# Three rounded passes for the recurrence's projections, their low halves taken by VectorE between the convolutions, and two smaller moves beside them

## The reference

```python
h = _rmsnorm(x, attn_norm_w[l])
(g_qkv, g_z, g_b, g_a, d_q, d_k, d_v, c_q, c_k, c_v, gate_raw) = _split_cols(h @ w_in[l])
y_a = _gdn_mixer(g_qkv, g_z, g_b, g_a, ...)   # short convolution over 5 tokens, silu, l2norm, gated delta rule
y_b = _diff_mixer(d_q, d_k, d_v, ...)         # two softmax maps a head, 4 heads
y_c = _gqa_mixer(c_q, c_k, c_v, ...)          # 8 heads of grouped-query attention
merged = (gates[:, :, 0] * (y_a @ w_branch_a[l]) + gates[:, :, 1] * (y_b @ w_branch_b[l])
          + gates[:, :, 2] * (y_c @ w_branch_c[l]))
x = x + merged @ w_out[l]
x = x + _hier_moe(_rmsnorm(x, ffn_norm_w[l]), ...)  # top-1 group, top-2 of 8 experts, 32 experts of 1024 x 512 x 3
```

## Time and profile before

| | |
|---|---|
| median of 3 runs | 1626.24 us (1624.73 to 1628.49) |
| the profiled execution's own time | 1625.27 us |
| its span, first to last instruction | 1623.4 us |
| mean granted TensorE clock | 0.956 of full speed |
| busy: PE, PEld, DVE, ACT, POOL | 81%, 61%, 41%, 29%, 7% of the span |
| moved by DMA | 490.60 MB, mean 302 GB/s |

### The profile page before, as it was taken

One profiled execution on the slowest core, in us unless ns is written; L12 is line 12 of the kernel. 1 busy time (PEld: TensorE's weight loads), 2 busy tenths in 40 slices (PEclk: granted clock), 3 DMA queues, 4 the chain that ended last, 5 costly groups with the idle time before them and its releaser, 6 DMA issues. The chain is left out here.

```text
span 1623.4 us, 46306 instructions
## 1 busy us (share of the span) xinstructions
PE 1312.4 (81%) x19436; PEld 996.8 (61%) x19437; DVE 665.4 (41%) x1598; ACT 469.3 (29%) x968; POOL 120.7 (7%) x108
## 2 busy tenths in 40 slices
PE   6998899987777766677789979998877776766665
PEld 5787787765554544455577867887655554454444
DVE  6657756653222111111286667666522221111112
ACT  3446745441111000101145466454401111100101
POOL 2002530000000000000010035200000000000000
PEclk9998999999999998999999989999999999999998
DMA  9441024588999999999964210445899999999996
GB/s 343 167 148 52 14 100 174 194 362 362 425 425 428 430 428 428 429 429 427 410 221 156 104 57 2 156 158 218 347 400 405 426 428 428 428 428 428 429 428 267
DMA packets 76747, 490.60 MB, mean 302 GB/s; under 512 B 12878, under 2 KB 15462, under 8 KB 52070
## 3 DMA queue, kind: packets, MB, share of 16 engines
q1 hardware_dynamic: 76646, 489.16, 74.1%
HBM read 488.09 MB, written 1.05 MB: 301 GB/s over the span
## 5 line engine op out<-in xcount | busy, mean ns | idle before, releaser
L1969 PE MATMUL ps<-ring,arena 128*32 128x128 f32 x5632 | 195.3, 296 | 82.1 <-DMA ring<-in_expert_w_gate_dram 69.6
L1969 PEld LDWEIGHTS ps<-ring,arena 128*32 128x32 f32 x5632 | 172.1, 120 | 114.0 <-DMA ring<-in_expert_w_gate_dram 73.4
L2047 ACT ACTIVATE arena<-ps 128x128 f32<-128x128 f32 x66 | 18.3, 277 | 522.2 <-PE ps L1969 522.2
L2184 DVE TENSOR_SCALAR arena<-cst,arena 128x128 f32 x132 | 39.8, 344 | 233.6 <-issue 228.1
L468 POOL TENSOR_TENSOR small<-small,cst 128x8 f32<-128x8 f32 (+1 forms) x21 | 27.7, 1321 | 1242.7 <-DVE small L715 456.2
L1969 PE MATMUL ps<-arena 128*32 128x128 f32 x2688 | 90.9, 291 | 35.8 <-DMA arena<-in_expert_w_gate_dram 31.7
L1969 PEld LDWEIGHTS ps<-arena 128*32 128x32 f32 x2688 | 80.2, 117 | 49.2 <-DMA arena<-in_expert_w_gate_dram 37.0
L1935 PE MATMUL ps<-xn,arena 128*32 128x256 f32 x1088 | 74.7, 390 | 42.3 <-DVE arena L2130 41.2
L1741 DVE TENSOR_TENSOR w_low<-ring,w_high 128x512 fp32r<-128x512 f32 x126 | 85.8, 706 | 52.1 <-ACT w_high L1672 52.1
L1991 PE MATMUL ps<-ring,arena 128*32 128x256 f32 x1440 | 89.6, 388 | 13.2 <-DMA ring<-in_expert_w_down_dram 12.9
L1672 ACT ACTIVATE w_high<-ring 128x512 fp32r<-128x512 f32 x126 | 77.2, 634 | 74.5 <-PE ps L1608 62.2
(11 more groups left out here) (361 smaller groups left out, 2496.9 us busy)
## 6 DMA issues: line engine op xcount, KB each, us to landing
ring<-in_expert_w_up_dram SPq DMA_DIRECT2D x44, 2048.0 KB, 39.2
ring<-in_expert_w_down_dram SPq DMA_DIRECT2D x44, 2048.0 KB, 39.7
ring<-in_expert_w_gate_dram SPq DMA_DIRECT2D x42, 2048.0 KB, 40.2
ring<-in_w_in_dram SPq DMA_DIRECT2D x28, 2048.0 KB, 8.1
arena<-in_expert_w_gate_dram SPq DMA_DIRECT2D x20, 2048.0 KB, 40.1
arena<-in_expert_w_up_dram SPq DMA_DIRECT2D x20, 2048.0 KB, 40.4
arena<-in_expert_w_down_dram SPq DMA_DIRECT2D x20, 2048.0 KB, 41.2
ring<-in_w_out_dram SPq DMA_DIRECT2D x4, 2048.0 KB, 7.9
```

The lines of the kernel that those rows point to most:

```text
L1969: ins = pe.matmul(bank_b[32 * g:32 * g + 32, u * P:(u + 1) * P], xg[:, c], spare[:, c, g] if from_tenth else w[:, u, c, g], start=(c == 0) ...
L2184: v.tensor_scalar(selw[:, t], bcast(cst[:, bass.ds(r * CAP + K_IOTA, CAP)].unsqueeze(1), [P, 4, CAP]), posn[:, t, bass.ds(e, 1)], weight[: ...
```

## The change

**1. Projections of the recurrence in three passes.** Each of the 12 heads of 128 columns gets its high half from ACT (`gdn_high`, 128x1024 elements), its low half from POOL (heads 0 to 3) or DVE (heads 4 to 11) (`gdn_low`), and PE does 24 rounded matmuls of 128x256 in place of 8 float32 ones. The high halves have four buffers. Heads 0 and 1 are prepared at the end of the projection block, 2 and 3 at the start of the next; the others by ACT behind the emptying of a piece and by DVE behind its convolution. `l2norm` is split, and the last two taps of v's convolutions come after the output copy of their step. **2. Beta and decay** become columns 256 to 271 of the `U_CKV` unit. **3. The low half of `HT`** is made once, in place; POOL's later four instructions for it go. **4. The sister's changes**: half of the transposes of `merged` come before the last chunk of the branch products, the other half after three chunks of the output product; the first three output weight chunks and the first half of `merged` are split into high and low before the barrier; the second half of the last merge is done behind it; SP's expert loads are reordered to suit.

```diff
-    wba = param(KC, 16)
+    KV_BA = 256 + 16
-    b_HT_lo = rounded("b_hT_low", "arena", 11008, KC, SEQ)
+    def gdn_high(act, l, i):
+        if i % HEADS == 0:
+            unit_landed(act, l, U_GQ + i // HEADS)
+        act.activation(g_hi[i % 4], gdn_columns(i), ACT.Copy).then_inc(d_hi, 1)
+    def gdn_low(eng, i):
+        eng.wait_ge(d_hi, i + 1)
+        eng.tensor_tensor(gdn_columns(i, low=True), gdn_columns(i), g_hi[i % 4].bitcast(F32),
+                          ALU.subtract).then_inc(d_lo if i < HEADS else d_lo_dve, 1)
...
-            if q == KC - 1:
-                pe.wait_ge(p_early, 16 * 3 * (l + 1))
-                for t in range(NT):
-                    for cc in range(KC):
-                        ins = pe.matmul(ps[6][:, t * 16:(t + 1) * 16], HT[:, cc, t * P:(t + 1) * P], wba[:, cc],
-                                        start=(cc == 0), stop=(cc == KC - 1))
...
                         for h in (2 * w, 2 * w + 1):
+                            i = HEADS * g + h
+                            if i < HEADS:
+                                pe.wait_ge(d_lo, i + 1)
+                            else:
+                                pe.wait_ge(d_lo_dve, i + 1 - HEADS)
                             for c in range(KC):
-                                ins = pe.matmul(bank[:, (h % 2) * SEQ:(h % 2 + 1) * SEQ],
-                                                unit8(U_GQ + g)[:, c, h * DH:(h + 1) * DH], HT[:, c],
-                                                start=(c == 0), stop=(c == KC - 1))
+                                pe.matmul(out, w_high[:, c], HT_hi[:, c], start=(c == 0), stop=False)
+                                pe.matmul(out, w_low[:, c], HT_hi[:, c], start=False, stop=False)
+                                ins = pe.matmul(out, w_high[:, c], HT_lo[:, c], start=False, stop=(c == KC - 1))
...
                     for piece in pieces:
                         empty(*piece)
+                        if piece[0] == "proj":
+                            pair = 2 * piece[1] + piece[2] + 2
+                            for i in range(2 * pair, min(2 * pair + 2, 3 * HEADS)):
+                                gdn_high(act, l, i)
...
-                work = {0: [(convolve, 0, 0), (convolve, 0, 1)], 1: [(convolve, 1, 0), (convolve, 1, 1)], 2: [(l2norm, 0)],
-                        3: [(convolve, 2, 0)], 4: [(convolve, 2, 1)], 5: [(l2norm, 1)]}
+                work = {0: [(convolve, 0, 0), (lows, 2), (convolve, 0, 1), (lows, 3)],
+                        1: [(convolve, 1, 0), (lows, 4), (convolve, 1, 1), (lows, 5)], 2: [(l2norm, 0)],
+                        3: [(convolve, 2, 0, range(3))], 4: [(convolve, 2, 1, range(3))], 5: [(l2norm, 1)]}
+                work_after = {2: [(l2scale, 0)], 3: [(convolve, 2, 0, range(3, TAPS))], 4: [(convolve, 2, 1, range(3, TAPS))], 5: [(l2scale, 1)]}
...
-                pool.wait_ge(d_fill, filled("proj", 2))
-                for j in range(4):
-                    pool.tensor_tensor(HT_lo[:, 2 * j:2 * j + 2], HT[:, 2 * j:2 * j + 2], HT_hi[:, 2 * j:2 * j + 2].bitcast(F32),
-                                       ALU.subtract).then_inc(f_hl, 1)
...
+                        if q == len(chunks) - 1:
+                            pe.wait_ge(f_m, 10)
+                            for cc in range(4):
+                                for t in range(NT):
+                                    ins = pe.transpose(ps[cc // 2][:, (cc % 2) * SEQ + t * P:(cc % 2) * SEQ + (t + 1) * P],
+                                                       merged[:, t, cc * P:(cc + 1) * P], ident)
+                            ins.then_inc(f_t, 1)
...
-                for n in range(RING, RING + 3):
-                    if n == RING + 2:
-                        sp.wait_ge(h_t, 4)
-                    load_expert(sp, l, n // 3, n)
+                load_expert(sp, l, SETS - 1, RING + 1)
+                sp.wait_ge(f_m, 12)
+                load_expert(sp, l, SETS - 1, RING)
+                sp.wait_ge(h_t, 2)
+                load_expert(sp, l, SETS - 1, RING + 2)
...
                 for q, (u, c) in enumerate(chunks):
-                    pe.wait_ge(h_ml, c // 2 + 1)
-                    pe.wait_ge(h_lo, q + 1)
+                    if q == 3:
+                        turn_merged()
+                    if c >= 2:
+                        pe.wait_ge(h_ml, c // 2)
+                    if q >= 3:
+                        pe.wait_ge(h_lo, q - 2)
```

More of the change, by code:

```diff
@@ L483, in encoder_trunk @@
     roped = 8
-    chunks_b = [(u, j, 256 if u == U_CKV else 512) for u in streamed_b for j in range(KC)]
+    chunks_b = [(u, j, KV_BA if u == U_CKV else 512) for u in streamed_b for j in range(KC)]
     used_at.update({u: (b_used, KC * (n + 1)) for n, u in enumerate(streamed_b)})
@@ L592, in w_high @@
                 unit_landed(act, l, u)
+                if u == U_CKV:
+                    act.wait_ge(p_early, 16 * 3 * (l + 1))
             if q >= 4:
@@ L624, in project_scalar @@
                         heads_out(2 * (n - 2) + t)
+        for i in range(2):
+            gdn_high(act, l, i)
         for t in range(NT):
@@ L758, in project_pool @@
         roots(pool, b_asked, b_root, [hrs[:, 0:8], hrs[:, 0:8], hrs[:, 0:2], hrs[:, 0:2]])
+        for i in range(2):
+            gdn_low(pool, i)
     with nc.Block() as block:
@@ L1023, in _, with convolve @@
                 v.tensor_scalar(gg, gg, -1.0, None, ALU.mult)
-                def convolve(g, w):
+                def convolve(g, w, taps=range(TAPS)):
                     v.wait_ge(d_empty, fills_at["proj", g, w] + 1)
@@ L1029, in convolve @@
                         v.wait_ge(d_fill, filled("tok", 0))
-                    for k in range(TAPS):
+                    for k in taps:
                         for h in (2 * w, 2 * w + 1):
@@ L1039, in convolve @@
                             link(ins)
-                    ins.then_inc(d_conv, 1)
+                        else:
+                            ins.then_inc(d_conv, 1)
                 def l2norm(g):
@@ L1674, in _ @@
                         f(*args)
+                unit_landed(act, l, U_OUT)
+                for c in range(3):
+                    act.activation(o_w_hi[:, c], unit8(U_OUT)[:, c], ACT.Copy).then_inc(f_hi, 1)
+                act.wait_ge(f_t, 4)
+                for q in range(2):
+                    act.activation(mergedT_hi[:, 2 * q:2 * q + 2].rearrange("p c t -> p (c t)"), ps[q][:, :], ACT.Copy).then_inc(f_yh, 1)
             @block.vector
@@ L1743, in _ @@
                         f(*args)
-                merge(2, 1)
+                for c in range(3):
+                    v.wait_ge(f_hi, len(chunks) + c + 1)
+                    v.tensor_tensor(w_lo[U_OUT % UNITS][:, c * 512:(c + 1) * 512], unit8(U_OUT)[:, c], o_w_hi[:, c].bitcast(F32),
+                                    ALU.subtract).then_inc(f_lo, 1)
+                v.wait_ge(f_yh, 4)
+                v.tensor_tensor(mergedT_lo[:, 0:2].rearrange("p c t -> p (c t)"), ps[0][:, :],
+                                mergedT_hi[:, 0:2].rearrange("p c t -> p (c t)").bitcast(F32), ALU.subtract).then_inc(f_yl, 1)
             @block.gpsimd
```

92 lines of the change are left out of this document (60 added, 32 removed).

## The result

The changed kernel takes 1639.9 us (median of 6 runs, 1633.6 to 1644.8) against 1625.5 for the kernel before (6 runs, 1620.5 to 1628.5): ratio 1.0088, 95% interval 1.0064 to 1.0112. The prediction was 1641 us, range 1630 to 1652. Two executions, one of the kernel before with 3133 us and one of a variant with 2102 us, lie far outside all others and enter no median and no interval. The profiled execution took 1640.1 us with a span of 1637.9, 14.5 us more than before; the prediction's sum was 14.6.

The account below looks back on a forecast made before the run. Expert loads bound the experts' part, engine latency the attention part, so delays before the tenth load move the end. 2 x (12.0 - 1.2 - 3.5) = +14.6 us on 1625.27 gives 1639.9, median 1641 us, range 1630 to 1652.

Parts of the forecast that it names:

- The new piece, 5.8 us: PE's recurrence projections: 48 rounded 128x256 matmuls at 0.12 us take 5.8 us, saving 1.2 us a piece if PE never waits.
- the third rival: Weight loads not hidden or clock never back: a three-pass piece costs 10.1 us, 1686 us in all; chance 0.04.
- First wait, 6.9 us: Attention block: PE asks for head 4's low half at 98.1 us, DVE ends it at 105.0, a 6.9 us wait.
- The low half, 1.23 us: DVE's 128x1024 low half of a head takes 1.23 us, from the nearest row with two inputs.
- Second wait, 9.4 us: Attention block: PE, through at 120.6 us, waits 9.4 us for head 8's low half, ready at 130.0 behind DVE's convolution.
- The restart, 1.4 us: After a gap PE runs 3.2 us at the lower clock level, priced at 1.4 us a restart.
- Copy of step 1, +12.0 us: Attention block: DVE's output copy of step 1 comes at 141.4 us instead of 129.41, 12.0 us late.
- Rest of the block, 0: Attention block behind the copy of step 1: no low half there, nothing taken, 2 us either way for the range.
- Beta and decay, -1.2 us: Projection block: float32 product goes, DVE's second rotary item starts earlier; 1.2 us a layer gained, bounds 0 and -3.6.
- heads 0 and 1 fall at the end of the projection block: hidden: POOL's low halves, 3.0 us a head, are hidden because ACT's last copies end later; if not, up to 1 us lost.
- The sister's changes, -3.5 us: Between last branch chunk and output product: reordered transposes and a 0.3 us barrier gain 3.5 us a layer, range -2 to -4.5.
- under 1 us: Sign for the tail: after the branches, PE's idleness at the barrier should be under 1 us.

## Why the prediction held, step by step

- **What bounds it.** Held here: a delay of 15.4 us before the tenth load of layer 1 moved the end by 14.5. It holds while the experts' part stays the same; where PE stopped in the first expert job, that part was 5.7 and 7.7 us longer.
- **The new piece, 5.8 us.** Held: neighbours start 0.12 us apart with a fresh weight load before each, so the loads are hidden, and the third rival, 10.1 us a piece, is out. The Trainium skill, TensorE: Matmul & The Clock Gate, Part 3 (The mechanism), lets a load overlap only when its row group differs, and this trace disagrees with that again; the same section also names the background weight buffer as a way to load ahead, which the prediction left out and which the 0.12 us would fit.
- **First wait, 6.9 us.** 7.00. Both of its ends came 1.4 to 1.5 us sooner than walked (asked at 96.6, ready at 103.6), since the first pieces began at 83.38 and ran at 2.4 GHz throughout.
- **The low half, 1.23 us.** 1.22 each, 2.35 for two in a row. The walk counts four of them in a step, as the kernel has them; the sign "step 0 longer by 2.5 us" at the prediction's end counts only two.
- **Second wait, 9.4 us.** 9.44. It follows from DVE's own row of steps alone, which the run with only the first wait removed confirms.
- **The restart, 1.4 us.** Mis-sized; this is what PE loses at the lower clock level after a wait. The lower level lasted 4.2 us behind the first wait (103.61 to 107.8), not 3.2, which is 4.2 x (1 - 0.12/0.21) = 1.8. From the second wait's end to the copy of step 1 it took 12.6 us instead of 11.4. "After a gap PE starts at the lower level" is true of these two waits and not of every one: behind the 2.81 us of the earlier trace rows the next matmuls last 0.28 us, as at the upper level.
- **Copy of step 1, +12.0 us.** +12.3 against the block's start in layer 0, +12.5 in layer 1. **Rest of the block, 0.** The block as a whole is 11.7 us longer in layer 0 (next block's first matmul at 179.04, before 167.26, starts 81.45 and 81.40), 12.4 in layer 1.
- **Beta and decay, -1.2 us.** Not resolved. Where PE had done the float32 product it now waits for DVE's low half behind the first rotary item, and less than before behind the second:

```profile
33.97 0.60 PE L571 MATMUL ps<-b_w_high,hT_high 128*128 128x272 f32 x1 [3.12 <-DVE w_low L726]
...
39.55 0.60 PE L571 MATMUL ps<-b_w_high,hT_high 128*128 128x272 f32 x1 [1.14 <-DVE w_low L726]
```

  DVE got through the rotary items 0.75 us sooner (39.07 for 39.82) and stood 0.87 ahead at 74.02. Then the step "heads 0 and 1 fall at the end of the projection block: hidden" failed: POOL's low half held DVE's last one for 2.2 us, PE waited 0.69, and the block of layer 0 ended where it had (81.45 for 81.40). In layer 1 it was 2.2 us shorter. But the same stretch, first three-pass matmul to the next block, with the same code took 66.2, 64.2 and 64.3 us in layer 0 of three profiles (the kernel before and the two with the sister's changes and float32 pieces), so a term of this size can't be read from one.
- **The sister's changes, -3.5 us.** -3.0 and -2.9. What was mis-sized is the barrier: PE stood 1.28 us there, not 0.3, and the sign "under 1 us" failed. The 0.3 was read where the block had waited for DVE's merge. By the trace the last one now is SP: DVE and PE were through by 338.9, but SP issues two expert loads that stand behind PE's last chunk, 0.80 us from 338.90 on, and the output product starts at 340.15. Before, the same two issues (326.47) were over while DVE still merged, until 329.22. No run moved them, so this is read from the rows and not tested. The cover of the last merge held (no idle time before 344.41).
- **The sum.** 14.6 predicted, 14.5 in the span: 12.4 a layer for 12.0 in the block's middle, 0.6 and 0 back in its rest, 0 and 2.2 for 1.2 in the projection blocks, 2.9 for 3.5 at the tail, and 1.6 us shorter experts' parts (0.7 and 0.9), which nobody forecast. The tenth load of layer 0 was 8.7 us late where half the sum had 7.3. The two waits, which carry the forecast, came as they were walked; that the total agrees to 0.1 us is luck, since the small errors cancel and single runs of a kernel spread over more.

## What to carry to other kernels

When a product gets a preparing step on another engine, price the place of that step in the engine's order before its length: here 128x8 instead of 128x1024 brought the tenth load of layer 1 forward by 5.3 us, and another place by 24.5. Walk both engines with the durations of the trace up to the first moment at which the consumer asks; what stands in front of the preparing step is the wait. When a wait goes, look where the gain disappears (here two steps later, behind ACT's order), and move that too.

## What the runs showed of the hardware

- A subtraction of DVE with two inputs took 2.88 us instead of 0.69 beside POOL's subtraction, and even its 128x4 operation took 1.03 us (83.94 us, L1035) where it takes 0.17 alone. The Trainium skill, SBUF — State Buffer, Who interferes with whom, says that a DVE instruction with two SBUF inputs contends with a GpSimd instruction that reads SBUF, and calls the shared port pair an exclusive lock. The trace agrees: POOL's first low half ran from 73.80 to 76.35, and DVE's subtraction, begun at 74.02, ended 0.55 us behind it. The prediction should have used this.
- PE stopped 1.91 and 2.09 us inside a row of equal matmuls in one program, in both of its profiles, and not in the one profile with eight matmuls a layer more ahead of it. The kernel before has one of 1.34 us at another place (397.44 us). The cause is open.
- PE's clock fell within a wait and stayed low behind it: granted 0.82 from 96 to 104 us, where PE stood 7.00 us, and matmuls 0.21 us apart until 107.8.
- Runs of the kernel before spread over 11 us (1619.5 to 1630.8), and single stretches of the same code differ by 2 to 3 us between layers and between profiles: from the copy of step 3 to the recurrence's first matmul it is 21.9 us in layer 0 and 24.6 in layer 1 of the kernel before, and 24.8 in layer 0 with the sister's changes alone, which don't touch it. In the changed kernel it is 21.9 and 25.1, and rows of eight weighted-sum matmuls in it last 1.00 us at some places and 1.81 at others, so part of it is the clock level.
